# Latent attention's end: the last two heads' output products in column halves, H's first turning between them, and a feed-forward weight split behind the last head

## The reference, cut to what matters

```python
for layer in range(DEPTH_2):
    h = _rmsnorm_2(x, norm_mix[layer])
    ...
        y = _mla_mixer(h, cos, sin, ...)      # returns o.reshape(B, S, heads * v_head) @ w_out
    x = x + y
    h = _rmsnorm_2(x, norm_ffn[layer])
    x = x + _conv_ffn(h, ffn_w_up[layer], ffn_conv_w[layer], ffn_conv_b[layer], ffn_w_down[layer])
```

## Time and profile before

| | us |
|---|---|
| median of 3 runs | 1552.59 |
| lowest, highest | 1550.44, 1556.13 |
| the profiled execution's own time | 1548.01 |
| its span | 1546.7 |
| PE busy, of the span | 1407.2 (91%) |
| DVE busy | 865.0 (56%) |
| ACT busy | 681.5 (44%) |

### The profile page before, as it was taken

One profiled execution on the slowest core, in us unless ns is written; L12 is line 12 of the kernel. 1 busy time (PEld: TensorE's weight loads), 2 busy tenths in 40 slices (PEclk: granted clock), 3 DMA queues, 4 the chain that ended last, 5 costly groups with the idle time before them and its releaser, 6 DMA issues.

```text
span 1546.7 us, 27421 instructions
## 1 busy us (share of the span) xinstructions
PE 1407.2 (91%) x11609; PEld 1189.8 (77%) x11609; DVE 865.0 (56%) x1546; ACT 681.5 (44%) x1185; POOL 10.6 (1%) x10
## 2 busy tenths in 40 slices
PE   7999999999989868768777799999999998899998
PEld 6999899899966434334343489999999986699997
DVE  6786463475522211212111478988988777588775
ACT  6544554544442111111110466565555566465553
POOL 1000000000000000000000100000000000000000
PEclk9999999999989997998998899999999999999999
DMA  7454354468799999999999744335565342446551
GB/s 239 146 171 148 120 172 132 155 224 326 297 412 424 426 424 422 425 426 425 426 426 425 283 153 134 109 126 193 173 207 182 108 150 74 145 149 206 191 178 68
DMA packets 170641, 372.05 MB, mean 241 GB/s; under 512 B 6912, under 2 KB 137088, under 8 KB 145936
## 3 DMA queue, kind: packets, MB, share of 16 engines
q1 hardware_dynamic: 170512, 370.22, 64.5%
HBM read 369.15 MB, written 1.05 MB: 239 GB/s over the span
## 4 chain that ended last, share of the span: by engine, by line
PE 63%; DMA 22%; DVE 7%; ACT 4%; issue 2%; SPq 1%; DVEq 0%; ACTq 0%
DMA wu<-in_expert_w_down_dram 17%; PE bank L602 16%; PE bank L603 16%; PE bank L604 16%; PE bank L1724 3%; DVE lo L566 2%; PE bank L1696 2%; DMA wu<-in_expert_w_up_dram 2%; PE bank L833 2%; PE bank L1762 2%; ACT hi L555 2%; PE bank L1776 1%; SPq L1295 1%; DMA raw<-in_w_in_dram 1%; PE bank L942 1%
## 5 line engine op out<-in xcount | busy, mean ns | idle before, releaser
L566 DVE TENSOR_TENSOR lo<-raw,hi 128x1024 fp32r<-128x1024 f32 (+2 forms) x315 | 376.4, 1216 | 175.6 <-ACT hi L555 174.7
L602 PE MATMUL bank<-XH,hi 128*128 128x256 f32 x1416 | 404.8, 286 | 7.4 <-DVE lo L566 3.7
L604 PE MATMUL bank<-XH,lo 128*128 128x256 f32 x1416 | 399.8, 282 | 0.0
L603 PE MATMUL bank<-XL,hi 128*128 128x256 f32 x1416 | 399.8, 282 | 0.0
L555 ACT ACTIVATE hi<-raw 128x1024 fp32r<-128x1024 f32 (+2 forms) x315 | 321.3, 1049 | 116.6 <-PE bank L604 68.1
L602 PEld LDWEIGHTS bank<-XH,hi 128*128 128x128 f32 x1416 | 270.4, 191 | 15.8 <-issue 11.5
L603 PEld LDWEIGHTS bank<-XL,hi 128*128 128x128 f32 x1416 | 270.5, 191 | 0.8
L604 PEld LDWEIGHTS bank<-XH,lo 128*128 128x128 f32 x1416 | 270.4, 191 | 0.0
L1724 PE MATMUL bank<-wu,xg 128*32 128x256 f32 x2048 | 166.1, 427 | 50.0 <-DMA wu<-in_expert_w_up_dram 46.8
L1724 PEld LDWEIGHTS bank<-wu,xg 128*32 128x32 f32 x2048 | 70.3, 119 | 122.7 <-DMA wu<-in_expert_w_up_dram 64.1
L1762 PE MATMUL bank<-wu,hidT 128*32 128x256 f32 x1024 | 74.5, 411 | 37.4 <-DMA wu<-in_expert_w_down_dram 26.7
(11 more groups left out here) (383 smaller groups left out, 2175.3 us busy)
## 6 DMA issues: line engine op xcount, KB each, us to landing
wu<-in_expert_w_gate_dram SPq DMA_DIRECT2D x64, 1024.0 KB, 26.6
wu<-in_expert_w_up_dram SPq DMA_DIRECT2D x64, 1024.0 KB, 26.3
wu<-in_expert_w_down_dram SPq DMA_DIRECT2D x64, 1024.0 KB, 26.9
raw<-in_w_in_dram SPq DMA_DIRECT2D x44, 1024.0 KB, 5.2
raw<-in_ffn_w_up_dram SPq DMA_DIRECT2D x44, 1024.0 KB, 5.0
raw<-in_ffn_w_down_dram SPq DMA_DIRECT2D x22, 1024.0 KB, 5.1
raw<-in_hgrn_w_in_dram SPq DMA_DIRECT2D x16, 1024.0 KB, 5.4
raw<-in_w_branch_ret_dram SPq DMA_DIRECT2D x8, 1024.0 KB, 7.2
```

The source lines that it names most:

```text
L566: dve.tensor_tensor(lo_of(u), v, hi_of(u), ALU.subtract).then_inc(*WL.inc(u))
L602: pe.matmul(dst, first[0], first[1], start=start, stop=False)
L603: pe.matmul(dst, second[0], second[1], start=False, stop=False)
L604: return pe.matmul(dst, third[0], third[1], start=False, stop=stop)
```

## The change

In PE's list the order at the end changes. Before, it was `out(6)`, `out(7)`, piece 0, piece 1. Now it is the blocks 0 and 1 of head 6, the blocks 0 and 1 of head 7, the blocks 2 and 3 of head 6, piece 0, the blocks 2 and 3 of head 7, piece 1. In ACT's list the high split of unit 10 moves from step 12 to step 13, behind `OH` of head 7. In DVE's list the low split of unit 10 moves behind `OL` of head 7 too, and the low split of unit 12 moves from behind the norm (line 791) to ahead of the sums. Also in DVE's list the `XL` instructions of piece 0 now stand between the sums 1 and 2.

```diff
-        O_HI = (0, 0, 1, 1, 3, 4, 5, 6, 7, 7, 9, 10, 11, 12, 13)
-        O_LO = (0, 0, 0, 0, 1, 3, 4, 5, 6, 7, 7, 9, 11, 11, 12)
+        O_HI = (0, 0, 1, 1, 3, 4, 5, 6, 7, 7, 9, 10, 10, 12, 13)
+        O_LO = (0, 0, 0, 0, 1, 3, 4, 5, 6, 7, 7, 9, 10, 12, 13)
...
-            def out(h):
+            def out(h, ns=range(4)):
 
                 u = unit2(O_TILE) + h
-                for n in range(4):
+                for n in ns:
...
             attend(7)
-            out(6)
-            out(7)
+
+            out(6, (0, 1))
+            out(7, (0, 1))
+            out(6, (2, 3))
             pe_piece(6, 0, X.dve)
+            out(7, (2, 3))
             pe_piece(6, 1, X.dve)
...
                 if t == 1:
                     X.dve.mark("H", 2 * c)
                     X.dve.mark("H", 2 * c + 1)
-            for p in range(4):
+                    dve_piece(6, c, "norm_ffn_2", 8)
+            for p in (2, 3):
                 dve_piece(6, p, "norm_ffn_2", 8)
```

## The result

The changed kernel took 1556.9 us as the median of 15 runs (1552.85 to 1560.69), the kernel before 1553.02 in 15 runs beside it (1550.02 to 1560.24). The ratio is 1.0024 with a 95% interval of 1.0013 to 1.0034: slower by 3.7 us, 2.0 to 5.3. That is a loss clear of the scatter, and one inside the prediction's bound of 0.5%, "the same".

What follows compares the result with a forecast made beforehand. PE, busy for 91% of the span, was taken to bound the kernel. The lost 2.66 us stall becomes a 5.3 us wait with half clock, net +2.05 us on the median 1552.59: 1554.6 us, range 1549.5 to 1559.

Steps and rivals of the forecast that it cites:

- bound of 0.5%: Whole kernel: about 0.5%, 7.8 us, is what a measurement can tell from no change; chance of "same" 0.94.
- The 2.66 us stall goes: PE ahead of head 7: its 2.66 us wait for OL disappears, and 18 matmuls run until about 1343.5.
- The wait moves to sum 0, behind unit 12's low split: PE ahead of piece 0: a wait of 5.3 us for DVE's sum 0, piece 0 starting at 1348.86.
- Half clock after the wait: PE behind the 5.3 us wait: clock at half up to piece 1's start, head 7's six matmuls 0.43 us each.
- my two bounds: Start of the turning of pieces 2 and 3: +0.85 us at full clock throughout, +2.8 at half clock up to it.
- rival 3: Feed-forward: half clock reaches into it, slower and clearly; 4 us more give +4, 1556.6 us; chance 0.12.
- activity releases the throttle: PE's clock: by the skill's rule a longer wait brings no recovery while PE idles, so +2.05 and not +0.85.
- The seam: From head 6's first output matmul to the turning of pieces 2 and 3: +2.05 us against before.
- the mark: Start of the second turning (pieces 2 and 3), behind unit 8's first four k: forecast 1355.2 against 1353.15.
- All of it is kept, since the feed-forward is bound by PE: Last feed-forward: PE waits once, 0.4 us, from 1355 us on, so time gained or lost before stays.
- The sum: Whole kernel: +2.05 us, a difference within one place, added to the median 1552.59 gives 1554.6 us.

Runs made afterwards that it cites:

- e1: The changed kernel with one number back, unit 12's low split again behind the norm; ratio to before 1.0004 (0.9991 to 1.0017).
- e5: The changed kernel with 20 matmuls more that nobody reads on PE, behind head 6's second half; one run only, 1553.57 us.
- e6: The changed kernel with all splits of units 10 to 12 moved behind the sums that they stood ahead of; ratio to before 0.9987 (0.9973 to 1.0001).
- e8: The kernel before, PE's order untouched, with DVE's sums ahead of the low splits of units 10 to 12; ratio 0.9989 (0.9973 to 1.0005).
- e2: The kernel before with only unit 10's two splits moved behind head 7's OH and OL; ratio to before 0.9978 (0.9966 to 0.999).
- e3: The kernel before with only unit 12's low split moved ahead of the sums; ratio to before 1.0011 (0.9999 to 1.0022).
- e4: The kernel before with only the changed orders of PE (halves of heads) and DVE's XL, both split tables as before; ratio 1.0032 (1.002 to 1.0045).
- before, again: The kernel before, unchanged, profiled a second time; from head 6's first output matmul to the turning of pieces 2 and 3 it took 12.06 us.

## Why the prediction was right, and where its size was off

The forecast was +2.0 us, a loss inside the bound of no change; measured are +3.7 (2.0 to 5.3). The bound itself was too coarse: 15 runs a side told the ratio to 0.1%, not 0.5%. Step by step:

- *The 2.66 us stall goes.* Right: no gap in the 18 matmuls.
- *The wait moves to sum 0, behind unit 12's low split.* Right, and shown by e1: with that split back, the wait shrinks from 4.83 to 3.09 us. Piece 0 was forecast 9.61 us after head 6's first matmul (1348.86 - 1339.25) and came after 9.28 and 9.44.
- *Half clock after the wait.* Right in both profiles, and e5 shows its price, 1.88 us behind the start of piece 0; my two bounds stood 1.95 apart (+0.85 and +2.8), the chosen value 1.2 above the lower. I let it end at the start of piece 1, and it lasted into unit 8's first matmuls. It did not go on into the rest (193.57 against 193.55), so rival 3, whose +4 us is nearer to the measured +3.7 than the forecast, is not what happened. The statement of the Trainium skill's page "TensorE: Matmul & The Clock Gate", part 1, that activity releases the throttle agrees with the rows here: the clock rose some 5 us after PE resumed and not in the wait.
- *The seam.* Forecast 15.95 (13.90 + 2.05), found 16.14 and 16.31. That it is this close is in part luck, since two misses cancel: piece 0 came 0.33 us earlier than forecast, and from piece 1 to the mark it took 3.42 us and not 2.9, with the clock at half for the first part of it.
- *All of it is kept, since the feed-forward is bound by PE.* Right: the rest is 193.51 to 193.61 us in every kernel that keeps the splits of units 10 and 11 ahead of the sums. e6 to e8 show where this ends: low splits put later start to hold `XL` or the gate's result, and 0.7 to 1.1 us are given back.

The term whose size is in doubt is the one in "The sum": "the term is a difference within one place, so I add it to the median". As a difference of the two first traces it is right (2.24 found, 2.05 forecast), and 2.0 is just the lower end of the timed interval. But the difference was taken against a trace of before in which the clock fell to half behind the 2.66 us stall. In another execution of the same kernel it had not, and the seam was 12.06. Against that the changed kernel's two profiles lose 4.1 and 4.25 us, against the first 2.2 and 2.4. The timed +3.7 lies between. Two profiles of the kernel before don't tell how often its clock falls; that the timed runs of before mix both lengths is argued from them and the timed ratios, and not shown run by run. The ratios do speak for a mix: with 12.06 as the seam of before, e2 would gain 0.85 us, less than its timed 1.6 to 5.3; with 13.90, e3 would gain 0.68 and e4 lose 2.3, against a timed -0.2 to +3.4 and +3.1 to +7.0. A mean near 13 fits these three and the changed kernel.

For the other rows only ranges can be compared. e2's seam is 0.85 to 2.69 under before and its time 1.6 to 5.3; e4's is 2.3 to 4.2 over, its time 3.1 to 7.0. For e6 to e8 seam and rest together are 203.5 to 203.9 us, against 205.65 and 207.45 in the two profiles of before, so 1.75 to 3.95 under it; the timed gains of 1.2 to 2.0 us have intervals that reach from about 4 us of gain to 1 us of loss. Whether they or e2 are the best is not settled; e2 alone is clear of no change.

## What to carry to other kernels

When an instruction is late because it stands behind a wait for a transfer, moving it ahead is right (e2), but look at what now stands behind that wait: here the residual sums, which PE needed next, were put behind one split more of a still later tile. Reordering PE's work into halves gives nothing while an engine that waits for DMA sets the end, and it takes away cover: the first half has less work to hide the next wait. A difference of a few microseconds should not be read from one trace if the place holds a stall behind which the clock may or may not fall; profile the kernel before more than once.

## What the runs showed of the hardware that was not expected

Behind stalls of nearly equal length PE's clock fell in one execution and not in others: with 2.66 us it fell to half (before), with 2.42 us (e3) and 2.40 us (before, again) it did not. The length doesn't decide it. All twelve profiles have another stall of this size at 53 us, long before anything that the edits touch: the clock fell to half in ten of them, behind 2.22 (e4), 2.31, 2.33, 2.35, 2.36 (changed), 2.39, 2.41, 2.47, 2.56 and 2.68 us (before, again), and did not behind 2.32 (e3) and 2.49 us (before). So the same stall of the same kernel fell in one profile and not in the other, here too, and the other way round than at the seam. What decides it is open.

At the seam it was worth 1.18 us in head 7's twelve matmuls (4.06 against 2.88) and 0.39 from the start of piece 0 to that of unit 8 (2.53 against 2.14), which with the stall's own 0.26 is the 1.84 us between two seams of one program. In the waits of 3.09 (e1), 3.94 (e4), 4.83 and 4.99 us (changed) the clock fell each time before PE resumed, and nearly all of the six or twelve matmuls of 512 columns behind them came at half pace.
